# GpSimd's head-weight multiply in a sparse-attention indexer: per-row scalar in place of a broadcast tensor

## The reference

```
r = jax.nn.relu(jnp.einsum('bqhe,ble->bqhl', qi, ki_all))   # 4 heads, 64 dims
score = jnp.einsum('bqhl,bqh->bql', r, wi)                  # one weight per query and head
score = jnp.where(adm, score, -jnp.inf)
_, idx = lax.top_k(score, topk)                             # 256
```

## Time and profile before

| | before |
|---|---|
| median of 3 runs (lowest to highest) | 5120.09 us (5118.19 to 5121.09) |
| profiled execution, first to last instruction | 5121.8 us |
| stage one ends (barrier) | about 2489 us |
| PE busy | 4351.6 us (85%) |
| DVE busy | 3484.2 us (68%) |
| ACT busy | 3455.7 us (67%) |
| POOL busy | 1618.2 us (32%), nearly all in stage one |

### The profile page before, as it was taken

One profiled execution on the slowest core, in us unless ns is written; L12 is line 12 of the kernel. 1 busy time (PEld: TensorE's weight loads), 2 busy tenths in 40 slices (PEclk: granted clock), 3 DMA queues, 4 the chain that ended last, 5 costly groups with the idle time before them and its releaser, 6 DMA issues. The chain is left out here.

```text
span 5121.8 us, 78325 instructions
## 1 busy us (share of the span) xinstructions
PE 4351.6 (85%) x26505; PEld 2716.9 (53%) x26505; DVE 3484.2 (68%) x6644; ACT 3455.7 (67%) x6887; POOL 1618.2 (32%) x1358
## 2 busy tenths in 40 slices
PE   6767778777677877777689999989999999989999
PEld 3334434443333433434366777767777777754444
DVE  1266778888797988989477777787776778625111
ACT  1578788888697787974378888868788885520100
POOL 1345556666647866677310000000000000000000
PEclk9888889888788888988799999999999999999999
DMA  6211111100011011101421111110110010044422
GB/s 143 61 51 45 38 38 36 35 33 36 22 44 39 33 37 44 42 32 46 152 70 56 51 42 39 40 53 31 34 40 28 28 40 24 12 119 134 118 94 103
DMA packets 201975, 276.98 MB, mean 54 GB/s; under 512 B 50496, under 2 KB 134176, under 8 KB 201056
## 3 DMA queue, kind: packets, MB, share of 16 engines
q1 hardware_dynamic: 198624, 271.81, 16.8%
q10 hardware_dynamic: 2960, 0.17, 0.0%
HBM read 156.73 MB, written 114.16 MB: 53 GB/s over the span
## 5 line engine op out<-in xcount | busy, mean ns | idle before, releaser
L595 PE MATMUL bank<-w,x 128*128 128x512 f32 (+1 forms) x2848 | 1256.8, 597 | 23.6 <-DVE w L940 13.5
L1042 DVE TENSOR_SCALAR_CACHE_REDUCE ties<-score,cand 128x512 int8<-128x512 f32 (+13 forms) x448 | 1110.6, 2479 | 123.2 <-POOL score L916 107.9
L595 PEld LDWEIGHTS bank<-w,x 128*128 128x128 f32 x2848 | 575.9, 206 | 612.7 <-issue 547.4
L806 ACT ACTIVATE act_junk<-score,a_cand,a_sign 128x384 int8<-128x384 f32 (+13 forms) x420 | 879.4, 2094 | 14.0
L1833 DVE CUSTOM_DVE_ANT_0 row<-bank,mask 128x512 f32<-128x512 f32 (+3 forms) x1024 | 622.6, 639 | 179.8 <-PE bank L1572 178.5
L613 PE MATMUL bank<-kiT,qi 128*128 128x512 f32 (+3 forms) x1136 | 395.3, 490 | 408.6 <-ACT relu L736 206.4
L1539 POOL TENSOR_TENSOR near_bias<-table,mask 128x2048 f32<-128x2048 f32 (+1 forms) x32 | 129.5, 4048 | 1763.9 <-DVE part L1833 1748.3
L1767 ACT ACTIVATE pT<-bank 128x512 f32<-128x512 f32 (+2 forms) x704 | 368.7, 524 | 426.2 <-PE bank L1588 424.0
L1669 ACT ACTIVATE row<-row,top 128x1024 f32<-128x1024 f32 (+7 forms) x640 | 632.8, 990 | 4.0 <-DVE top L1846 4.0
L1588 PE MATMUL bank<-ident,row 128*128 128x128 f32 x4224 | 593.7, 281 | 26.4 <-DVE pT L1944 19.5
L1572 PE MATMUL bank<-kT,qb 64*128 64x256 f32 (+1 forms) x4352 | 608.4, 396 | 8.7 <-DVE part L1833 5.4
(11 more groups left out here) (255 smaller groups left out, 4882.6 us busy)
## 6 DMA issues: line engine op xcount, KB each, us to landing
qk_t<-ring SPq DMA_DIRECT2D x66, 256.0 KB, 2.0
gates<-ring SPq DMA_DIRECT2D x66, 256.0 KB, 2.0
gate<-gates SPq DMA_DIRECT2D x33, 512.0 KB, 3.4
out<-x_in SPq DMA_DIRECT2D x33, 512.0 KB, 2.9
x<-in_x_prompt SPq DMA_DIRECT2D x32, 512.0 KB, 3.7
mixed<-mixT SPq DMA_DIRECT2D x64, 256.0 KB, 2.1
mix_in<-mixed SPq DMA_DIRECT2D x32, 512.0 KB, 4.2
x_in<-in_x_prompt SPq DMA_DIRECT2D x32, 512.0 KB, 3.8
```

The costliest lines, as they stand in the source:

```text
L595: ins = pe.matmul(p_bank[n % 2][:, 0:n1 - n0], held[:, c * P:(c + 1) * P], w[:, c, n0:n1], start=(c == 0), stop=(c == KC - 1))
L806: tick(act.activation(junk, row, ACT.Sign, bias=c, scale=back, accum_out=a_sum[:, :]))
L1042: n = tick(dve.tensor_scalar(ties[:, 0:width], row, c.bitcast(F32), 0.0, ALU.is_ge, ALU.add, accum_out=counts[:, i:i + 1]))
```

## The change

In `add_scores` the weight is no longer spread over n columns as a second tensor of a tensor_tensor multiply; the multiply is a tensor_scalar whose scalar is the one-column pointer `weight[:, u % 2, h:h + 1]`. The adds, the waits, the order and every other engine's program stay.

```diff
-                        r, weighs = relu[at % 3][:, 0:n], weight[:, u % 2, h:h + 1].to_broadcast([P, n])
+                        r, weighs = relu[at % 3][:, 0:n], weight[:, u % 2, h:h + 1]
                         pool.wait_ge(s_rl, at + 1)
                         if h == 0:
                             pool.wait_ge(s_wi, u + 1)
-                            pool.tensor_tensor(to, r, weighs, ALU.mult).then_inc(s_pa, 1)
+                            pool.tensor_scalar(to, r, weighs, None, ALU.mult).then_inc(s_pa, 1)
                         else:
-                            k = tick(pool.tensor_tensor(r, r, weighs, ALU.mult))
+                            k = tick(pool.tensor_scalar(r, r, weighs, None, ALU.mult))
                             pool.wait_ge(s_pool, k)
                             pool.wait_ge(s_pa, at)
                             pool.tensor_tensor(to, to, r, ALU.add).then_inc(s_pa, 1)
```

## The result

The changed kernel is slower: median 5288.27 us (5285.17 to 5292.79, 4 runs) against 5120.59 us (5118.19 to 5126.60, 4 runs), ratio 1.0325 with a 95% interval of 1.031 to 1.0339. The loss is 168 us. The forecast was 60 us faster. Of its cases it was the first rival, a slow new form, that came true; the prediction gave it a chance of 0.30. All profiles here are of one core, and the profiled span after is 5284.2 us.

A forecast was written before the change was run, and what follows sets the result against it. No engine was full in stage one; waits, with POOL's latency inside a burst, decide. ACT's waits for L907 (32 to 41 us), L912 (25) and DVE's for L916 (4 to 8), less 8, gave 60 us: 5060 us, range 5020 to 5350.

The forecast's parts named there:

- the first rival: Same 568 POOL multiplies: pointer form slower than 1.04 us each; 5470 us at 2.2 us, 5250 at 1.6; chance 0.30.
- step (b): Price of POOL's new multiply at 512 columns: 0.73 us, 0.31 us less for each undisturbed one.
- The steep line through the two short rows: Upper price bound from POOL's 1- and 20-column tensor-scalar rows: 3.95 ns a column, 2.2 us at 512 columns.
- The pointer: Fetching the scalar in POOL's new multiply: 0.06 us, taken from DVE's pointer against immediate form.
- The sentence on the Trainium skill's figure: POOL multiply at 769 ns at best for 512 elements: 0.27 us saved each, some 52 us in all.
- Step (c): Which saved POOL time in stage one reaches the end through waits: sum 61 to 74 us.
- its counts: Stage-one waits taken to shrink: 133 of ACT for L907, 82 for add L912, 13 of DVE for L916.
- the 8 us held back: Some 8 us deducted for what ACT's evacuations behind TensorE's projections and late DVE keep.
- the floor: First rival's least loss, from 142 h3 waits and 82 L912 waits: 262 us at 2.2 us, 131 at 1.6.
- The no-change rival: POOL's multiply stays at 0.95 to 1.1 us, or is faster and DVE keeps its pace: 5115 us, chance 0.14.
- Much faster: Multiplies freed beside DVE's scan in late odd tiles: 45 us more, about 5010 us; chance 0.06, within faster.
- the slow case: Sign: multiplies above 1.04 us, POOL's late share rising from 65% toward full, ACT's L907 waits growing by the excess each.

The follow-up runs named there:

- the copy: Kernel before with POOL's multiplies L907 and L909 replaced by plain copies, head weights left out of the score: 5045.66 us, ratio 0.9842.
- the run with L907 alone: Only head 0's multiply L907 (142 of 568) in the new form, the rest as in the kernel before: 5174.3 us, ratio 1.0089.
- the late tiles: New form only for tiles 21 to 31 (312 of 568 multiplies), earlier tiles as in the kernel before: 5241.8 us, ratio 1.0225.
- the fourth buffer: Four relu buffers instead of three, space from narrower scratch rows: 5224.77 us on the changed kernel, 5094.95 us on the kernel before.

## Why the prediction was wrong

The result lies inside the range that the prediction held for 8 in 10 (5020 to 5350 us), but only by the part of it that belongs to the first rival.

**The price of the new form, step (b), is the step that failed.** It took 0.73 us, "the copy's slope from the 20-column row", because "the streams are those of a copy and a difference over 19 columns can be start-up". The runs show 1.56 us. The copy itself is what it was taken for (0.61 us at 512 columns; the 396 ns row gives a slope of 0.80 and not 0.82 ns, which moves it by 0.01 us), but a tensor-scalar operation is not a copy with arithmetic for nothing: 0.86 ns a column for the copy, 2.5 with one operation, 3.35 with two. The steep line through the two short rows, which gave 2.2 us, was the better warning, though it erred in the other direction: 3.95 ns a column between 1 and 20 columns, 2.5 between 128 and 512; why the short rows rise faster is not shown. The value lay between the stated ends, and the chosen one at the wrong end: the rows nearest to the new instruction by their form were the two short tensor-scalar rows, and the argument left their slope for that of another operation.

**The pointer,** put at 0.06 us from DVE's 214 against 154 ns, measures 0.07 us on POOL. This was near, and small.

**The sentence on the Trainium skill's figure** (769 ns for 512 elements in a tight loop at best, "GPSIMD Engine Reference", section 3.1) gave the same sign as the forecast. The runs show 1490 ns for this engine's tensor-scalar with a constant, so that figure is no price of this instruction; the copy, at 611 ns, even lies below it.

**Step (c), what lies on the path,** gives the right sum for a shorter multiply, but not by its terms. For the copy its counts give 133 x 0.24 to 0.43 and 82 x 0.43 and 13 x 0.43 to 0.86, together 73 to 104 us, less the 8 us held back; 81 us were measured. The waits themselves moved otherwise: ACT's for L907 fell by 31 us (32 to 57 by the count), those for the add by 99 us (35 by the count) and DVE's for L916 by 27 us (6 to 11), and TensorE then stood 46 us longer for the indexer keys, where 8 us had been held back. That the errors cancel is luck. For the longer multiply the same counts give 133 x 0.52 and 82 x 0.52 and 13 x 0.52 to 1.04, together 119 to 125 us, and the 168 us lie well above. The bounds of the stage were read rightly: the loss lies wholly before the barrier. That every such saved or added microsecond passes one wait undiminished does not hold; the run with L907 alone kept 48 of the 72 us by which that wait grew.

**The first rival** had the place, the sign and the threshold. Its price was short at the measured length: "the floor gives 131 us, 5250 us" for 1.6 us, where 1.56 us gave 5288 us. The floor at 0.52 us excess is 142 x 0.52 + 82 x 0.52 = 116 us; it keeps the count of 82 waits for the add, which in fact became 131. Its 350 us for an excess of 1.17 us were short too: 0.955 us of excess already gave 319 us, and the share of 0.59 measured there would make 665 us of added POOL time some 390 us, an estimate. The picture behind it, POOL becoming the bound late, was in part right: POOL rises only to 76% in the late stretch, and the late tiles hand on 72%, but in the last tile's step it is all but full. The same columns, the kernel before first:

```profile
2376.00:2464.00 88.00, 72.51 (x180) 37.59 (x180) 72.77 (x50) 24.33 (x43) 83.54 (x59) 0.83 0.16 58
```
```profile
2538.00:2624.00 86.00, 56.00 (x135) 27.42 (x134) 57.53 (x38) 18.64 (x32) 84.25 (x48) 0.76 0.14 53
```

That is 95% before and 98% after, and the last tile's eight units take 99.8 us after (2524.3 to 2624.2) and 87.2 us before.

**The no-change rival** offered "POOL's loop, not its inputs, sets the 1.66 ns a column". For one-input work the time does rise with the operations, 0.61 us with none, 1.56 with one and 2.00 with two, only at a higher price than supposed. Its other remark, that the broadcast operand reads cheaper, holds against another full tensor (1.04 against 1.28 us), not against the same tile twice.

**Much faster:** not seen. The one-input multiply stands beside DVE's scan (which reads `ties` as both of its inputs) as the two-input one did; DVE and POOL after, in order of time:

```profile
2578.68 9.09 DVE L971 TENSOR_TENSOR_SCAN score<-ties 128x3840 f32<-128x3840 int8 x1
...
2579.74 9.39 POOL L907 TENSOR_SCALAR score<-relu,weight 128x512 f32<-128x512 f32 x1
```

That agrees with the Trainium skill's "SBUF — State Buffer", section "Who interferes with whom": one SBUF read by GpSimd is enough for the collision.

The prediction took DVE's two-input work as what disturbs POOL. The traces show that its one-input work just before the scan does so too; DVE and POOL before, then after:

```profile
2428.27 3.23 DVE L969 TENSOR_SCALAR ties<-score,cand 128x3840 int8<-128x3840 f32 x1
2429.44 2.95 POOL L907 TENSOR_TENSOR score<-relu,weight 128x512 f32<-128x512 f32 x1
```
```profile
2573.39 3.25 POOL L909 TENSOR_SCALAR relu<-relu,weight 128x512 f32<-128x512 f32 x1
2573.96 2.22 DVE L968 TENSOR_SCALAR mask<-score,cand 128x3840 bf16<-128x3840 f32 x1
```

L968 and L969 have one tensor input and a pointer scalar; the multiplies beside them took 2.95 us in place of 1.04 and 3.25 us in place of 1.56. Undisturbed, both would have ended before the scan began (2431.53 and 2578.68 us).

Of the signs that the prediction named, the one for the slow case held: ACT's wait for L907 grew with 126 waits by 84 us, 0.7 us each beside the excess of 0.52 us.

## What to carry to other kernels

In these runs fewer operands were not less time on POOL: price an elementwise instruction by its own form at its own width, and if the only rows of that form are short, weigh their slope more than the slope of another form. In this kernel, whose engines were 65 to 89% busy and hand work round through a few buffers, a lengthened step cost about half its added time and a shortened one returned less, so the total busy time was a poor guide in either direction. To price a cure, measure it on both kernels: the fourth buffer gave 69 us on the changed one, but 31 of them on the kernel before as well. Those 31 us, bought with scratch columns that nobody used, are more than any form of the multiply measured here gave, as the one that the kernel had is the cheapest that multiplies by the weight.

## What the runs showed of the hardware that was not expected

- POOL, float32, ns a column between 128 and 512 columns: copy 0.86; tensor-tensor with a broadcast column or with the same tile twice 1.7; tensor-tensor with two different full tiles 2.1 (451 and 1275 ns); tensor-scalar 2.5; tensor-scalar with two operations 3.35.
- A pointer scalar on POOL costs 0.07 us an instruction over a constant, at 128 columns (597 against 523 ns) as at 512 (1562 against 1490 ns).
- POOL reads one tile as both operands as cheaply as a broadcast column (1.04 us at 512 columns, 1.28 us with another full tile). Why the same tile is cheap was not tried further, and it stays open what in the loop makes one scalar operation dearer than a broadcast tensor.
- POOL is held up beside one-input work of DVE too: a multiply took 2.95 us in place of 1.04 beside a tensor-scalar of 3840 columns on DVE, and 3.25 us in place of 1.56 in the changed kernel.
